# Hybrid encoder block: residual stream stored ahead of the last layer, final tiles accumulated into it in DRAM

## What is computed

```python
def reference(x, ...):
    h = rmsnorm(x, ffn1_pre_norm)
    x = x + 0.5 * rmsnorm(swiglu(h, w_ffn1_in, w_ffn1_out), ffn1_post_norm)

    h = rmsnorm(x, mix_pre_norm)
    x = x + rmsnorm(hybrid_mixer(h, ...), mix_post_norm)

    h = rmsnorm(x, ffn2_pre_norm)
    x = x + 0.5 * rmsnorm(swiglu(h, w_ffn2_in, w_ffn2_out), ffn2_post_norm)
    return x
```

## Time and profile before

| | |
|---|---|
| median of 3 runs | 1575.42 us (1573.7 to 1576.45) |
| profiled execution: its time | 1571.19 us |
| profiled execution: its span | 1569.4 us |
| TensorE matmul busy | 1511.2 us (96%) |
| VectorE busy | 753.8 us (48%) |
| ScalarE busy | 584.5 us (37%) |
| GpSimd busy | 23.5 us |
| mean granted TensorE clock | 0.988 of full speed |
| transfers | 138.70 MB, 88 GB/s |

### The profile page before, as it was taken

How to read it: one execution, slowest core, us unless ns; L and a number is a source line. 1 busy time by engine, 2 the same in 40 slices (tenths; PEclk the granted TensorE clock), 3 DMA queues, 4 the chain that set the end, 5 groups by cost and what they waited for, 6 DMA issues and landing times. The chain is left out here.

```text
span 1569.4 us, 20232 instructions
## 1 busy us (share of the span) xinstructions
PE 1511.2 (96%) x7546; PEld 1234.7 (79%) x7546; DVE 753.8 (48%) x1158; ACT 584.5 (37%) x861; POOL 23.5 (1%) x29
## 2 busy tenths in 40 slices
PE   7999999999999999999999989999998999999996
PEld 5888888887987777777877777777785888888885
DVE  5444444224744444533357776764436444443223
ACT  5322323223533444443245654453335322333221
POOL 0000000000100000000000000000000000000001
PEclk9999999999999999999999999999999999999998
DMA  4323222232422222122222121122221223222222
GB/s 168 101 97 104 94 94 94 95 101 73 145 88 85 91 67 91 56 68 90 98 72 67 63 70 63 67 68 81 94 93 55 94 95 101 99 94 94 94 94 81
DMA packets 39185, 138.70 MB, mean 88 GB/s; under 512 B 4535, under 2 KB 4535, under 8 KB 39095
## 3 DMA queue, kind: packets, MB, share of 16 engines
q1 hardware_dynamic: 37440, 132.14, 24.9%
q0 software_dynamic: 1552, 5.82, 1.3%
q10 hardware_dynamic: 144, 0.04, 0.0%
HBM read 135.81 MB, written 2.17 MB: 88 GB/s over the span
## 5 line engine op out<-in xcount | busy, mean ns | idle before, releaser
L257 PE MATMUL ps<-hh,whi 128*128 128x512 f32 x1280 | 512.4, 400 | 20.6 <-DVE hl L519 12.4
L258 PE MATMUL ps<-hl,whi 128*128 128x512 f32 x1280 | 502.0, 392 | 0.0
L259 PE MATMUL ps<-hh,wlo 128*128 128x512 f32 x1280 | 501.6, 392 | 0.0
L247 ACT ACTIVATE whi<-raw 128x1024 fp32r<-128x1024 f32 x242 | 256.0, 1059 | 626.0 <-PE ps L259 562.7
L252 DVE TENSOR_TENSOR wlo<-raw,whi 128x1024 fp32r<-128x1024 f32 x242 | 296.1, 1224 | 376.1 <-ACT whi L247 376.1
L257 PEld LDWEIGHTS ps<-hh,whi 128*128 128x128 f32 x1280 | 242.2, 189 | 82.7 <-issue 19.2
L259 PEld LDWEIGHTS ps<-hh,wlo 128*128 128x128 f32 x1280 | 242.1, 189 | 51.9
L258 PEld LDWEIGHTS ps<-hl,whi 128*128 128x128 f32 x1280 | 242.7, 190 | 48.6 <-issue 0.5
L257 PE MATMUL ps<-ah,whi 128*128 128x512 f32 x352 | 138.4, 393 | 0.8 <-DVE tmp L364 0.8
L258 PE MATMUL ps<-al,whi 128*128 128x512 f32 x352 | 137.6, 391 | 0.0
L259 PE MATMUL ps<-ah,wlo 128*128 128x512 f32 x352 | 137.3, 390 | 0.0
(11 more groups left out here) (217 smaller groups left out, 1584.5 us busy)
## 6 DMA issues: line engine op xcount, KB each, us to landing
raw<-in_wstream SPq DMA_DIRECT2D x244, 512.0 KB, 3.2
bias<-vec_dram POOLq DMA_DIRECT2D x8, 576.0 KB, 7.0
xt<-in_x_t SPq DMA_DIRECT2D x8, 256.0 KB, 6.0
out_t<-xt SPq DMA_DIRECT2D x8, 256.0 KB, 2.0
cst<-in_consts POOLq DMA_DIRECT2D x1, 704.0 KB, 5.1
hot_sb<-in_onehot POOLq DMA_DIRECT2D x1, 297.0 KB, 4.1
vec_dram<-vec_sb POOLq DMA_DIRECT2D x1, 72.0 KB, 2.9
par<-in_params ACTq DMA_DIRECT2D x1, 40.5 KB, 3.8
```

The lines of the kernel that those rows point to most:

```text
L247: nc.scalar.activation(whi[:, s, :], raw[:, s, :], ACT.Copy).then_inc(head_done, 1)
L257: nc.tensor.matmul(out, w, m, start=start, stop=False)
L258: nc.tensor.matmul(out, w, ml, start=False, stop=False)
L259: return nc.tensor.matmul(out, wl, m, start=False, stop=stop)
```

## The change

- Once `post2 x` has counted 8, GpSimd issues one transfer that stores the whole of `xt` to the output (2 MB), and waits for its completion.
- For each tile, as soon as its scaled tile is there, GpSimd issues a transfer from `scaled_y[d]` to the tile's rows of the output that adds to what is there (`accum_op=ALU.add`), then waits for all eight.
- The additions on GpSimd and VectorE, SP's eight stores and SP's waits are gone; so is `POOL_SUMS`.

```diff
-POOL_SUMS = 5
...
             with sp.Fori(1, N_PAIRS) as pair:
                 load_block(sp, pair, 0)
                 load_block(sp, pair, 1)
-            for d in range(KT):
-                if d < POOL_SUMS:
-                    sp.wait_ge(sem("out_pool"), d + 1)
-                else:
-                    sp.wait_ge(sem("out_dve"), d + 1 - POOL_SUMS)
-                sp.dma_start(out_t[d * P:(d + 1) * P, :], xt[:, d, :]).then_inc(sem("stored"), 16)
-            sp.wait_ge(sem("stored"), 16 * KT)
...
-            for d in range(POOL_SUMS):
+            pool.wait_ge(*counted("post2", "x", KT))
+            pool.dma_start(out_t.rearrange("(d p) n -> p d n", p=P), xt[:]).then_inc(sem("residual_out"), 16)
+            pool.wait_ge(sem("residual_out"), 16)
+            for d in range(KT):
                 pool.wait_ge(*counted("post3", "scaled", d + 1))
-                nc.gpsimd.tensor_tensor(xt[:, d, :], xt[:, d, :], scaled_y[:, d, :], ALU.add
-                                        ).then_inc(sem("out_pool"), 1)
+                pool.dma_start(out_t[d * P:(d + 1) * P, :], scaled_y[:, d, :], accum_op=ALU.add
+                               ).then_inc(sem("stored"), 16)
+            pool.wait_ge(sem("stored"), 16 * KT)
...
-            for d in range(POOL_SUMS, KT):
-                dve.wait_ge(*counted("post3", "scaled", d + 1))
-                nc.vector.tensor_tensor(xt[:, d, :], xt[:, d, :], scaled_y[:, d, :], ALU.add
-                                        ).then_inc(sem("out_dve"), 1)
```

## The result

| | before | changed |
|---|---|---|
| median (7 runs each) | 1575.85 us (1570.58 to 1577.38) | 1583.14 us (1578.47 to 1584.03) |
| ratio | | 1.0049, 95% interval 1.0034 to 1.0063 |
| profiled execution: span, clock | 1569.4 us, 0.988 | 1581.4 us, 0.983 |

What follows compares the result with a forecast made beforehand. The matmul stream bounds the kernel (TensorE busy 1511.2 of 1569.4 us), plus stretches where TensorE has nothing to do. Join 0 and tail +2.4 us took the median from 1575.42 to 1577.8 us (+0.15%); range 1572.5 to 1588.0.

Steps and rivals of the forecast that it cites:

- rival 2: Tail: slow read and write back, three passes per accumulating transfer instead of two; +7.6 us, 1583.0 us; chance 0.27.
- t0 to first bytes: Tail, from the first scaled tile's end: GpSimd starts 0.09 us later, bytes flow 0.9 us after that.
- movement of 2 MB: Tail: eight accumulating transfers, two fetches each through the path, 1.31 us each, 10.5 us together.
- last byte to landing: Tail: 1.5 us from last byte to completion, read from a software store of 72 KB.
- landing to end: Tail: program ends 0.4 us after the last landing, as after SP's stores in the kernel before.
- The join: Between second residual sum and last feed-forward layer: the 2 MB store fits an idle transfer window; cost 0.
- Rival 3: Join: the residual store holds up the weight stream; +2.7 us, 1578.1 us without the tail, about 1580.5 with it; chance 0.04.
- Half the rate: Tail: accumulating transfers fetch tile and output through the path, about 200 GB/s of output; +2.4 us.
- Its own signs of being wrong: Tail: landing times don't grow, an accumulating transfer moves below 200 GB/s, or GpSimd takes over 0.66 us to issue one.
- the lower end of -3.6 us: Tail: accumulating transfers cost as plain stores, -2.6 us, or -3.6 with the smallest software transfer's 2.4 us.
- Rival 1: Tail: plain rate, the output's fetch overlaps the tile's; -2.6 us, 1572.8 us; chance 0.21.
- rival 4: Tail: the change moves nothing because storing 2 MB bound it anyway; 1575.4 us; chance 0.04.

Runs made afterwards that it cites:

- the early store alone: Kernel before plus only the 2 MB store of the residual stream at the join, with later additions and stores waiting for it; ratio 1.0004.
- the plain stores from the same queue: Changed kernel with plain stores in place of the accumulating ones, same GpSimd queue and waits, last addition left out; ratio 0.9983 to the kernel before.
- the sum in SBUF: Changed kernel with the eight transfers adding into xt, SP storing each sum, no early store; end 19.0 us after the first scaled tile's end.
- one transfer: Changed kernel with a single accumulating transfer of 2 MB behind all eight scaled tiles; executed once, end 21.7 us after the first scaled tile's end.
- SP as the waiter: Changed kernel with only the last wait, for all eight transfers, moved from GpSimd to SP; ratio 1.0038 to the kernel before.
- without additions: Kernel before without the last additions, SP storing the scaled tiles themselves; ratio 0.9962.
- the kernel with two transfers: Kernel before with tiles 0 and 1 by early store and accumulating transfer, GpSimd adding 2 to 4, VectorE 5 to 7; ratio 0.9993.
- the third adder: Kernel before with TensorE adding tiles 1 and 3, copied out by ScalarE, GpSimd and VectorE the rest; ratio 0.9999, with SP's stores reordered 0.9991.

## Why the prediction was right and where it fell short

The time lay inside the range, but not inside the forecast's own one (1576.8 to 1579.5): the likeliest case, +0.15% and within 0.2%, was too low, 0.49% were measured. What held the time in the wide range was the room left for rival 2 and for transfers with little overlap, and neither came; so the direction and the half rate were foreseen, and that the range held is in part luck. Against the terms of the sum, from t0:

| term | predicted | changed kernel |
|---|---|---|
| t0 to first bytes | 1.1 us | 2.0 |
| movement of 2 MB | 10.5 | 12.1 |
| last byte to landing | 1.5 | 0.9 |
| landing to end | 0.4 | 2.2 |
| t0 to end | 13.5 | 17.2 |

- **The join: right.** The store took 0.90 us of GpSimd, its bytes 5 us, and the stretch behind it stayed at 360.75 us. Rival 3 is refuted by the early store alone.
- **Half the rate: right.** A full path with 205 GB/s of output against 399 and, in the plain stores from the same queue, 373 to 406. The Trainium skill's rule (Collectives: The Full Stack, section "The bandwidth ceiling: the fold count and why AG ≠ RS ≠ AR"), stated for ReduceScatter against AllGather, gives a reducing transfer half a copy's rate; the trace agrees, 399 / 205 = 1.9. That a second fetch is the reason remains an inference: the sum in SBUF shows that it isn't DRAM, but an adding unit of half the speed would look alike.
- **The movement: mechanism right, size short by 1.6 us.** The term took the flat rate from the first byte on. With the output in DRAM there is a slow start (80 GB/s over 1.4 us) and then a stretch of several us below 185 GB/s (141 in the row at 1569.60, 150 to 167 with one transfer), and with the sums in SBUF less than half as much is lost. Its cause is open.
- **First bytes: short by 0.9 us.** I let GpSimd start a transfer 0.09 us after its release, the figure of its add. Measured are 1564.81 - 1564.22 = 0.59 us, which the chain books as issue ahead of the instruction, and 1.4 us more to the first bytes, where the prediction had 0.9 from its row of a plain store; in the plain-store kernel they are 1.1.
- **The end: short by 1.8 us.** The 0.4 us were SP's, and the prediction carried them over to a kernel in which GpSimd waits last. This was the largest miss and had no bounds: it was copied, not costed. SP as the waiter ends the program 0.6 us earlier in all.
- **Rival 2 (+7.6) is close to the result by its size, not by its mechanism.** It wanted a third pass, so a flat 133 GB/s; the flat part runs at 205.
- **Its own signs of being wrong.** Landing times do grow, from 4.1 to 10.1 us. The rate falls below 200 GB/s in the slow stretches, so this sign did come. GpSimd's transfer instructions last 1.99 us at the median instead of 0.55, but they start 0.54 to 0.66 us apart, so issue held nothing up. The 0.13 of the forecast's chance that was to come in part from issue at up to 1.04 us had no ground: issue at 1.04 us stays hidden behind movement at 1.31. And the lower end of -3.6 us let 256 KB land in the 2.4 us of a transfer of 3 KB; with 0.65 us for its bytes it is -2.9.
- **One reading of the kernel before was wrong.** VectorE did not stand still for 1.67 us at 1563.91: the line below shows it in its second add. That this add is slow because GpSimd adds beside it is what the times suggest; it doesn't enter the sum, which starts at 1558.43.

```profile
1563.83 1.75 DVE L1595 TENSOR_TENSOR xt<-xt,scaled_y 128x512 f32<-128x512 f32 x1
```

- **Rival 1 and rival 4** fall with the landing times that grow to 10.1 us, and with the tail of 7.1 us without additions.

The bound of 0.2% was close to the forecast (+2.4 of 3.15 us), so two missed fixed costs were enough to carry it over.

## What to carry to other kernels

Moving an addition into a transfer saves engine time only where the transfer path has room for a rate of half; in a tail where a plain store already takes as long as a tile, it turns a term of 0.66 us per 256 KB into 1.3 to 1.5. When a program's last work moves to another queue, cost the whole way anew: release to issue, issue to first byte, last landing to the end. And read a tail from a mark just ahead of it: the two spans differed by 12.0 us, of which 5.9 had arisen before the change's first instruction.

## What the runs showed of the hardware

- Transfer instructions on GpSimd overlap: eight of 0.93 to 2.80 us start 0.6 us apart and fill 7.12 us together; plain ones take 0.54 us each. The time for which one holds the engine is read from the next start (0.54 to 0.60 us between the first four, 0.65 us in the kernel with two transfers), not from its duration.
- The page's count of DRAM reads is 135.81 MB before and after, although the changed kernel has 2.1 MB of output to read back; the fetch of an accumulating transfer isn't in it. The written count goes from 2.17 to 4.27 MB.
- A plain store of 256 KB by the software queue lands in 2.9 us at the median, one by SP's in 2.0. The Trainium skill (DMA: Bandwidth & Descriptors, section "Anatomy of one DMA — SWDGE (gpsimd) path") gives a fit of 2.0 us plus bytes at 436 GB/s, an estimate of 2.6 us here; the trace has 2.3 to 3.0.
- With the third adder, TensorE's granted clock was 1.00 in the stretch from 1562.5 to 1565.2, in which it was idle (its last matmul had ended at 1562.4), 0.53 from 1565.2 to 1567.2 and 0.50 to 1568.7, while it worked on tile 1, and 1.00 again from 1568.7. A float32 matmul of 128x512, two instructions, took 1.0 us at the upper level and 1.8 to 2.1 us around the lower.
